# Attention projections on one core: two kv heads' keys in one tile, ten query and key tiles instead of twelve

## The reference

```python
proj = h @ w_in
q, k, v, xbc, z, dt_raw = jnp.split(proj, list(IN_SPLITS), axis=-1)
q = apply_rope(q.reshape(bsz, s, N_KV_HEADS, Q_PER_KV, HEAD_DIM), cos, sin) * (HEAD_DIM ** -0.5)
k = apply_rope(k.reshape(bsz, s, N_KV_HEADS, HEAD_DIM), cos, sin)
v = v.reshape(bsz, s, N_KV_HEADS, HEAD_DIM)
attn_out = mixture_of_dilations(q, k, v).reshape(bsz, s, ATTN_WIDTH)
```

## Time and profile before

| | us |
|---|---|
| median of 3 runs (2406.78 to 2408.15) | 2407.63 |
| the profiled execution | 2409.64 |
| its span, first to last instruction | 2407.9 |
| PE busy in it | 2284.5 (95%) |
| DVE busy | 1762.8 (73%) |
| ACT busy | 847.5 (35%) |
| POOL busy | 224.3 (9%) |

### The profile page before, as it was taken

One profiled execution on the slowest core, in us unless ns is written; L12 is line 12 of the kernel. 1 busy time (PEld: TensorE's weight loads), 2 busy tenths in 40 slices (PEclk: granted clock), 3 DMA queues, 4 the chain that ended last, 5 costly groups with the idle time before them and its releaser, 6 DMA issues. The chain is left out here.

```text
span 2407.9 us, 29647 instructions
## 1 busy us (share of the span) xinstructions
PE 2284.5 (95%) x10470; PEld 1863.1 (77%) x10470; DVE 1762.8 (73%) x2675; ACT 847.5 (35%) x1300; POOL 224.3 (9%) x188
## 2 busy tenths in 40 slices
PE   7999999999999999999999787998999999999996
PEld 6888888888878777778778565887788888888885
DVE  8877777777588878877573477777787777777766
ACT  6322222222344655556223443212432222222222
POOL 0000000000001333323000245400000000000000
PEclk9999999999999999999999888999899999999998
DMA  4111111112331010101112322312411111111122
GB/s 152 53 53 52 52 52 52 52 52 78 105 115 45 18 36 18 36 18 36 44 44 96 124 79 87 97 46 86 140 48 53 52 52 52 52 52 52 48 96 105
DMA packets 52326, 155.62 MB, mean 65 GB/s; under 512 B 5904, under 2 KB 7952, under 8 KB 50064
## 3 DMA queue, kind: packets, MB, share of 16 engines
q1 hardware_dynamic: 52240, 154.51, 19.4%
HBM read 133.18 MB, written 21.30 MB: 64 GB/s over the span
## 5 line engine op out<-in xcount | busy, mean ns | idle before, releaser
L1009 DVE TENSOR_TENSOR acc<-psum,acc 128x512 f32<-128x512 f32 x288 | 197.9, 691 | 160.7 <-PE psum L595 158.0
L593 PE MATMUL psum<-act_hi,tile_hi 128*128 128x512 f32 x704 | 276.9, 393 | 11.9 <-DVE acc L617 7.1
L594 PE MATMUL psum<-act_lo,tile_hi 128*128 128x512 f32 x704 | 275.7, 392 | 0.0
L595 PE MATMUL psum<-act_hi,tile_lo 128*128 128x512 f32 x704 | 275.6, 391 | 0.0
L708 ACT CAST t_hi<-t_raw 128x512 fp32r<-128x512 f32 x144 | 89.8, 624 | 308.3 <-DVE t_raw L869 295.0
L593 PEld LDWEIGHTS psum<-act_hi,tile_hi 128*128 128x128 f32 x704 | 133.4, 189 | 41.9 <-DVE acc L617 9.5
L595 PEld LDWEIGHTS psum<-act_hi,tile_lo 128*128 128x128 f32 x704 | 133.3, 189 | 28.0
L594 PEld LDWEIGHTS psum<-act_lo,tile_hi 128*128 128x128 f32 x704 | 133.5, 190 | 27.5
L1853 DVE TENSOR_TENSOR probs_t_lo<-psum,probs_t_hi 128x512 fp32r<-128x512 f32 x144 | 96.8, 686 | 55.1 <-ACT probs_t_hi L1779 55.1
L730 ACT ACTIVATE sum<-sum 128x512 f32<-128x512 f32 x72 | 45.7, 635 | 245.8 <-DVE sum L963 151.2
L454 PE MATMUL psum<-norm_hi,plain_hi 128*128 128x512 f32 x288 | 112.0, 389 | 0.0
(11 more groups left out here) (373 smaller groups left out, 5741.2 us busy)
## 6 DMA issues: line engine op xcount, KB each, us to landing
tile_lo_raw<-in_d SPq DMA_DIRECT2D x40, 512.0 KB, 4.3
gate_raw<-in_gu SPq DMA_DIRECT2D x36, 512.0 KB, 4.0
up_raw<-in_gu SPq DMA_DIRECT2D x72, 256.0 KB, 3.6
raw_tile<-in_w_xz SPq DMA_DIRECT2D x19, 512.0 KB, 3.6
gate_up_lo_raw<-in_gu SPq DMA_DIRECT2D x8, 1024.0 KB, 5.1
cum_rows<-cum_scratch SPq DMA_DIRECT2D x8, 1024.0 KB, 4.8
raw_tile<-in_w_out SPq DMA_DIRECT2D x16, 512.0 KB, 3.6
raw_tile<-in_w_att SPq DMA_DIRECT2D x11, 512.0 KB, 3.5
```

Source lines behind the costliest of these rows:

```text
L593: pe.matmul(o, w_h[:, s, d, :], a_h[:, s, x], start=(s == 0), stop=False)
L594: pe.matmul(o, w_h[:, s, d, :], a_l[:, s, x], start=False, stop=False)
L595: mm = pe.matmul(o, w_l[:, s, d, :], a_h[:, s, x], start=False, stop=(s == 1))
L1009: v.tensor_tensor(x, banks(4 + d % 4), x, ALU.add).then_inc(sem(p + "_acc"), 1)
```

## The change

A kv group no longer has a key tile of its own. The even groups have three tiles, and their third holds the keys of two kv heads: 64 columns of head g on partitions 0 to 63 and 64 columns of head g + 1 on partitions 64 to 127. The odd groups have two tiles, for their queries; their keys are already in slot 2 of `q_k_next`. So there are ten tiles and not twelve, and the weights on the host are ten tiles. `k_hi` and `k_lo` still hold a head's keys on both halves of the partitions: each is now written in two steps of 64 partitions instead of one of 128, the second of them across partitions. A group has six steps `qk_hi` and `qk_lo` instead of five, and the first scores of a group wait for three of them instead of two. All counts of semaphores follow.

```diff
-        NEXT_TILES = [(g, t) for g in range(1, KVH) for t in range(3)]
+        TILES = [(g, t) for g in range(KVH) for t in range(2 if g % 2 else 3)]
+        NEXT_TILES = TILES[3:]
+        THROUGH = [1 + max(n for n, (f, _) in enumerate(TILES) if f == g) for g in range(KVH)]
...
-                        add("POOL", "cos", ("cos", f, h), 1.33, ("piece", f, h), ("qk_lo", g - 1, 4))
+                        add("POOL", "cos", ("cos", f, h), 1.33, ("piece", f, h), ("qk_lo", g - 1, 5))
...
-                for n in range(5):
-                    add("ACT", "qk", ("qk_hi", g, n), 1.05, ("sin", 3 * g - 1, 1) if g else ("first_sin", 2, 1),
+                for n in range(6):
+                    add("ACT", "qk", ("qk_hi", g, n), 1.05, ("sin", THROUGH[g] - 4, 1) if g else ("first_sin", 2, 1),
...
-                    ("max", *SCORES[n - 2]) if n > 1 else None, ("qk_lo", g, hh + 1) if i == 0 else None,
+                    ("max", *SCORES[n - 2]) if n > 1 else None, ("qk_lo", g, hh + 2) if i == 0 else None,
...
             if n == 0:
-                act.wait_ge(sem("at_sum"), 6 * g + 6)
+                act.wait_ge(sem("at_sum"), 2 * THROUGH[g])
...
-                act.copy(kh[:], qn[:, 2, :]).then_inc(sem("at_qk_hi"), 1)
+            if n < 2:
+                act.copy(kh[own(g + n), :], qn[own(g), 2, :]).then_inc(sem("at_qk_hi"), 1)
...
-            if n == 0:
-                v.tensor_tensor(kl[:], qn[:, 2, :], kh[:].bitcast(F32), ALU.subtract).then_inc(sem("at_qk_lo"), 1)
+            if n < 2:
+                v.tensor_tensor(kl[own(g + n), :], qn[own(g), 2, :], kh[own(g), :].bitcast(F32), ALU.subtract)\
+                 .then_inc(sem("at_qk_lo"), 1)
...
-        kg = w_in[:, k0 + g * HD:k0 + (g + 1) * HD]
-        att += [q_tiles[2 * g], q_tiles[2 * g + 1], col_tiles(np.concatenate([kg, kg], 1), 0, 1)[0]]
+        att += [q_tiles[2 * g], q_tiles[2 * g + 1]]
+        if g % 2 == 0:
+            att.append(col_tiles(w_in, k0 + g * HD, 1)[0])
```

More of the change, by code:

```diff
@@ L1467, in mixer_plan @@
                         add("DVE", "pieces", ("piece", f, h), 0.69, last[f], row[h])
-                        add("POOL", "cos", ("cos", f, h), 1.33, ("piece", f, h), ("qk_lo", g - 1, 4))
+                        add("POOL", "cos", ("cos", f, h), 1.33, ("piece", f, h), ("qk_lo", g - 1, 5))
                     else:
-                        add("DVE", "pieces", ("piece", f, h), 0.69, last[f], ("qk_lo", KVH - 1, 4))
+                        add("DVE", "pieces", ("piece", f, h), 0.69, last[f], ("qk_lo", KVH - 1, 5))
                     bank = ("piece", f, h)
@@ L1524, in piece_pe @@
             t, rotated, h = n // 4, n % 4 >= 2, n % 2
-            w = 3 * g + t
+            w = TILES.index((g, t))
             x = slice(h * HALF, (h + 1) * HALF)
@@ L1528, in piece_pe @@
             if rotated or tiles[0] == 0:
-                wait(pe, "pj_read", 12 * g + n)
+                wait(pe, "pj_read", 4 * w + n % 4)
             if rotated:
@@ L1546, in staged_pe @@
                 if n == 0:
-                    pe.wait_ge(sem("pj_read"), 12 * KVH)
+                    pe.wait_ge(sem("pj_read"), 4 * len(TILES))
                 wait(pe, "xz_read", n)
                 if t == 0:
-                    pe.wait_ge(sem("at_w_lo"), 3 * KVH + 1)
+                    pe.wait_ge(sem("at_w_lo"), len(TILES) + 1)
                 else:
@@ L1680, in score @@
                 if i == 0:
-                    pe.wait_ge(sem("at_qk_lo"), 5 * g + 2 + hh)
+                    pe.wait_ge(sem("at_qk_lo"), 6 * g + 3 + hh)
                 wait(pe, "at_max", n - 1)
@@ L1751, in qk_hi @@
                 wait(act, "at_score", 32 * g)
-                act.copy(kh[:], qn[:, 2, :]).then_inc(sem("at_qk_hi"), 1)
-            else:
-                act.copy(qst[own(n - 1), n - 1, :], qn[own(n - 1), (n - 1) // 2, :]).then_inc(sem("at_qk_hi"), 1)
+            if n < 2:
+                act.copy(kh[own(g + n), :], qn[own(g), 2, :]).then_inc(sem("at_qk_hi"), 1)
+            else:
+                hh = n - 2
+                act.copy(qst[own(hh), hh, :], qn[own(hh), hh // 2, :]).then_inc(sem("at_qk_hi"), 1)
         def qk_lo(v, g, n):
-            v.wait_ge(sem("at_qk_hi"), 5 * g + n + 1)
-            if n == 0:
-                v.tensor_tensor(kl[:], qn[:, 2, :], kh[:].bitcast(F32), ALU.subtract).then_inc(sem("at_qk_lo"), 1)
+            v.wait_ge(sem("at_qk_hi"), 6 * g + n + 1)
+            if n < 2:
+                v.tensor_tensor(kl[own(g + n), :], qn[own(g), 2, :], kh[own(g), :].bitcast(F32), ALU.subtract)\
+                 .then_inc(sem("at_qk_lo"), 1)
             else:
-                hh = n - 1
+                hh = n - 2
                 v.tensor_tensor(qst[own(hh + 1), hh, :], qn[own(hh), hh // 2, :], qst[own(hh), hh, :].bitcast(F32),
@@ L1825, in piece_dve @@
             x = slice(h * HALF, (h + 1) * HALF)
-            m = 2 * (3 * g + t)
-            v.wait_ge(sem("pj_mm"), 12 * g + n + 1)
+            w = TILES.index((g, t))
+            m = 2 * w
+            v.wait_ge(sem("pj_mm"), 4 * w + n % 4 + 1)
             if rotated:
@@ L1858, in staged @@
                 if n == 0:
-                    v.wait_ge(sem("at_qk_lo"), 5 * KVH)
+                    v.wait_ge(sem("at_qk_lo"), 6 * KVH)
                 v.wait_ge(sem("xz_mm"), n + 1)
@@ L1901, in piece_pool @@
                 x = slice(h * HALF, (h + 1) * HALF)
-                gp.wait_ge(sem("pj_read"), 12 * g + n + 1)
-                wait(gp, "at_qk_lo", 5 * g)
+                gp.wait_ge(sem("pj_read"), 4 * TILES.index((g, t)) + n % 4 + 1)
+                wait(gp, "at_qk_lo", 6 * g)
                 gp.tensor_tensor(qn[:, t, x], qr[:, x], cos[:, x], ALU.mult).then_inc(sem("at_cos"), 1)
```

6 lines of the change are left out of this document (3 added, 3 removed).

## The result

The changed kernel takes 2417.73 us in the median of 11 runs (2413.50 to 2426.03), the kernel before 2408.59 us beside it (2406.78 to 2410.88, 11 runs). The ratio is 1.0036, 95% interval 1.0027 to 1.0045: **9.1 us slower**, where the prediction said 2414 us and the sum +6.3.

What follows compares the result with a forecast made beforehand. PE was taken to bound the attention, its holes filled with parts of tiles. Removed work -26.0, rotation waits -0.5, changes of group +25.0, bare stretch +5.7 and group 3's end +2.1 gave +6.3 us: 2414 us, range 2396 to 2427.

Steps and rivals of the forecast that it cites:

- the sum +6.3: Whole kernel: the prediction's terms added up, -26.0 - 0.5 + 25.0 + 5.7 + 2.1 us, meaning slower.
- Removed work, -26.0: PE in the attention: 32 projection parts (21.8 us) and four rotations (4.2 us) gone, 26.0 us less work.
- The waits at the changes of group: PE waits for DVE's six subtractions in a row: 9.1, 9.1 and 9.7 us, plus 1.0 behind the first two.
- its own sign: One stated sign of a wrong prediction: waits at the changes of group shorter than 8 us.
- POOL's stretch: At the first two changes of group, one POOL scaling beside DVE's subtractions lengthens them by 0.8 us.
- The clock, 2.45 us each, net +4.9: Behind each of three long waits PE runs 5 us at 1.2 GHz, losing 2.45 us; kernel before loses it once.
- The rival by which the lower clock lasts longer: Behind the waits 1.2 GHz holds twice as long, 2.45 us more per change: 2424 us; 13% for more than +16.
- The bare stretch, +5.7: Group 2, units 4 to 7, without parts: PE waits 7 us where the kernel before waits 1.3.
- The end of group 3, +2.1: Stretch without parts at group 3's end grows from 9 to 13 blocks, 0.52 us of waits each.
- The extra cast in group 0, nothing: Group 0's first scores come 1.24 us later, under six to eight ready PE parts, so no cost.
- The rivals of a full and of a smaller gain: Full gain: 26.5 us faster, 2381 us, 7%. Smaller gain: short waits, clock kept, 2396 us, 21% for -12 to -5.

Runs made afterwards that it cites:

- experiment 2: Changed kernel plus 28 unread matmuls on PE in each of the three long waits at the changes of group: 2418.76 us, ratio 1.0037.
- experiment 5: Changed kernel with POOL's scan product held behind DVE's two mixing products, plus 28 unread matmuls per long wait: 2410.89 us; or plus 16 repeated projection parts: 2414.34 us.
- the run with the scan's edit: Changed kernel with POOL's product of a scan chunk waiting until DVE's two mixing products of that chunk are done: 2413.55 us, ratio 1.0023.
- experiment 1: Planner gives key and query casts and subtractions last rank: changed kernel with it 2391.37 us, ratio 0.9930; kernel before with it 2399.12 us, ratio 0.9960.

## Why the prediction was right

Time, sign and the main mechanism were right. The price of the clock was not, and part of the sum's nearness is luck. By its own terms:

- **Removed work, -26.0.** Right: 25 to 25.5 us of PE's work at full clock (experiment 2). PE has 104 records fewer, as forecast: 100 matmuls, of which the four rotations are two records each.
- **The waits at the changes of group.** Right in place, releaser and length: 9.1, 9.1 and 9.7 us and 1.0 each for the first two's rotations, 29.9 us, against 8.04, 7.79, 7.63 with 0.96, 1.31 and 1.48 beside them, 27.2 us. (For the third the terms named add up to 11.4 us of DVE, not 11.6.) Two of the three single waits, 7.79 and 7.63, lie just under the 8 us below which the prediction called itself wrong, so by its own sign it had them a little too long. What it had as one wait at the third change came as two, since the transposes there already wait for a low part. POOL's stretch was 0.81 us for 0.8. The rule of the Trainium skill (SBUF — State Buffer, "SBUF: two separate sides") that was weighed there, by which one scaling holds DVE for its whole 1.1 us, gives 0.3 us more than this row shows.
- **The clock, 2.45 us each, net +4.9.** The fall came as said, and it made PE's busy time longer by half of 12.1 us against half of 5.0 before, +3.5. As a price it was over-sized: it costs 0, 0 and 2.7 us at the three changes (experiments 2 and 5). The step that was left out is the wait behind the wait: at the first two changes PE waits for DVE again, so what it loses to the clock it would have waited. Less the 2.45 of the kernel before, whose price no run tests, the net is near nothing where +4.9 was forecast. The rival by which the lower clock lasts longer behind sparse work fell: it lasted 3.5, 2.8 and 5.8 us. But its condition did not come about either, for PE worked without a gap through all three stretches; the work is sparse only once the clock is up again. So these waits do not test what the Trainium skill (TensorE: Matmul & The Clock Gate, "Part 1: The HAM clock gate") says of sustained activity, by which this rival was weighed; they agree with it in so far as the clock rose each time in the middle of such work.
- **The bare stretch, +5.7.** PE is idle for 8.7 of 34 us there against 7 forecast. Right in kind, 1.7 us too small; that PE's work is not what mostly sets the pace there was shown by experiment 5 (10.9 us more of it cost 2.8).
- **The end of group 3, +2.1.** Idle time rose from 4.7 us of 16 to 7.5 of 25: +2.8.
- **The extra cast in group 0, nothing.** The first score came 0.6 us later, 768.97 against 768.35; within what executions differ in (768.04 to 769.76 in the profiles of the same attention code).

By PE's time the terms made -26.0 of work, +4.9 of clock and +27.4 of waits, and the profile of the attention has -25.5, +3.5 and +30.5, +8.5 us in all for the 8.6 measured. Of the waits, those at the changes were put 2.7 us too high, the bare stretch and the end of group 3 together 2.4 too low; 1.4 are the DMA wait of this one execution, and 2 us stand at no place that was named. Clock too high and waits too low make up for each other in part, and the +9.1 of the medians holds a spread of 12 us between executions that the sum says nothing about. So the order of size was worked out, and the last 2 us of nearness are luck. The rivals of a full and of a smaller gain fell with the long waits, but they were not far off as designs: one line in the planner makes the full gain and more.

## What to carry to other kernels

Work taken off the busiest engine is worth little where that work was the filler between other engines' results (10.9 us put back there cost 2.8): ask of each removed instruction what the engine would have waited for in its place. Where an order is planned from costs, look at blocks of one kind of step that nobody needs at once; here their rank was worth 26 us, three times what the change cost. A slower clock costs nothing where the engine waits again right behind it; ask that of each place. After an edit compare also the stages behind it: a scan with the same code differed by up to 7 us between executions, as much as the effect that was looked for in the attention.

## What I had not expected of the hardware

- DVE's products from SBUF and POOL's, started together, hold each other up: 4.07 us for two mixing products against 2.36, and 4 us of busy time saved on each of the two engines when a wait keeps them apart. POOL's product takes 1.90 us by itself (1435.00 in the run with the scan's edit) and 2.94 beside them, and the two of DVE were 1.71 longer beside it, nearly all of it. The Trainium skill (SBUF — State Buffer, "SBUF: two separate sides") has such instructions lock each other out for the whole of one; this pair agrees, the scaling beside the key subtractions (0.81 of 1.12 us) less so.
- The granted clock also falls where PE does not stand still, and not in every execution of the same code. The kernel before, and the run of experiment 5 with the extra matmuls, have 0.50 from 684.9 to 688.3, ahead of the attention, with PE busy all through; the changed kernel, with the same steps there, has 1.00. The run of experiment 1 has three such stretches in its attention, of some 3.4 us each. One of them:

```profile
784.00:787.00 3.00, 3.00 (x9) 2.37 (x8) 2.93 (x13) 2.21 (x6) 1.36 (x3) 0.50 0.04 16
```

  What brings them on no run here shows.
- PE came back to full clock in the middle of gapless work, behind all three waits of the changed kernel (at 857.7, 963.5 and 1062.5), after 3.5, 2.8 and 5.8 us at the lower one.
